# A mixture-of-experts layer on one core: expert rows through tables in DRAM instead of one-hot matmuls

## The reference

```
logits = xf @ w_router
vals, idx = lax.top_k(logits, 2)
gates = sum(one_hot(idx, 8) * softmax(vals))
for e in range(8):
    out += gates[:, e:e+1] * ((silu(xf @ wg[e]) * (xf @ wu[e])) @ wd[e])      # inner width 3584
```

## Time and profile before

| | |
|---|---|
| median of 3 runs | 1660.03 us (1659.11 to 1660.29) |
| profiled execution, first to last instruction (span) | 1658.4 us |
| PE busy | 95% of the span |
| DVE, ACT, POOL busy | 72%, 58%, 3% |
| mean granted clock of PE | 0.974 |
| moved by DMA | 431.69 MB, mean 260 GB/s |

### The profile page before, as it was taken

The page is one execution under the profiler, slowest core; times in us unless marked ns, Lnnn a source line. Parts: engine busy times, 40 slices in busy tenths (PEclk is TensorE's granted clock), DMA queues, the critical chain, the costliest instruction groups (busy, mean ns, idle before and its releaser), DMA issues.

```text
span 1658.4 us, 22346 instructions
## 1 busy us (share of the span) xinstructions
PE 1580.2 (95%) x8017; PEld 1306.1 (79%) x8017; DVE 1192.4 (72%) x1088; ACT 961.0 (58%) x932; POOL 56.3 (3%) x90
## 2 busy tenths in 40 slices
PE   4899899999799699999999999999999999999996
PEld 3687699999687478878888888887887887887885
DVE  3635455544545468879879879879878887987886
ACT  4534444334335357757766766766766775776674
POOL 2010000000210100000000000000000000000001
PEclk9999899999799779999999999999999999999999
DMA  8433254440524059979979978979997997997992
GB/s 326 148 127 118 86 183 172 159 172 29 229 105 165 0 218 367 370 274 351 370 280 346 364 298 334 365 292 339 365 356 273 365 366 280 349 365 283 349 365 107
DMA packets 60618, 431.69 MB, mean 260 GB/s; under 512 B 6913, under 2 KB 7327, under 8 KB 8975
## 3 DMA queue, kind: packets, MB, share of 16 engines
q1 hardware_dynamic: 59966, 429.53, 68.6%
q0 software_dynamic: 608, 1.56, 0.3%
HBM read 428.60 MB, written 2.74 MB: 260 GB/s over the span
## 4 chain that ended last, share of the span: by engine, by line
PE 92%; DVE 4%; ACT 2%; issue 1%; POOL 1%; DMA 0%; POOLq 0%; DVEq 0%; SPq 0%; ACTq 0%
PE bank L265 28%; PE bank L267 27%; PE bank L266 27%; PE bank L1437 4%; PE bank L1461 1%; PE bank L1111 1%; DVE wlo L253 1%; ACT whi L249 1%; PE bank L1481 1%; ACT junk L438 1%; PE bank L1483 1%; DVE hT_lo L700 0%; ACT hT_hi L447 0%; DVE xn L693 0%; PE bank L1238 0%
## 5 line engine op out<-in xcount | busy, mean ns | idle before, releaser
L253 DVE TENSOR_TENSOR wlo<-raw,whi 128x2048 fp32r<-128x2048 f32 x402 | 920.5, 2291 | 209.2 <-ACT whi L249 208.9
L249 ACT ACTIVATE whi<-raw 128x2048 fp32r<-128x2048 f32 x402 | 769.0, 1915 | 189.7 <-PE bank L267 189.3
L265 PE MATMUL bank<-whi,gT_hi 128*128 128x512 f32 x896 | 365.1, 408 | 0.0
L267 PE MATMUL bank<-whi,gT_lo 128*128 128x512 f32 x896 | 355.4, 397 | 0.0
L266 PE MATMUL bank<-wlo,gT_hi 128*128 128x512 f32 x896 | 354.1, 395 | 0.0
L267 PEld LDWEIGHTS bank<-whi,gT_lo 128*128 128x128 f32 x896 | 169.2, 189 | 39.3
L265 PEld LDWEIGHTS bank<-whi,gT_hi 128*128 128x128 f32 x896 | 169.9, 190 | 36.0
L266 PEld LDWEIGHTS bank<-wlo,gT_hi 128*128 128x128 f32 x896 | 169.9, 190 | 34.8
L265 PE MATMUL bank<-whi,eT_hi 128*128 128x512 f32 x448 | 177.4, 396 | 1.0 <-DVE eT_lo L991 1.0
L266 PE MATMUL bank<-wlo,eT_hi 128*128 128x512 f32 x448 | 177.2, 396 | 0.0
L267 PE MATMUL bank<-whi,eT_lo 128*128 128x512 f32 x448 | 176.3, 393 | 0.0
(11 more groups left out here) (187 smaller groups left out, 1632.6 us busy)
## 6 DMA issues: line engine op xcount, KB each, us to landing
raw<-in_stream SPq DMA_DIRECT2D x402, 1024.0 KB, 4.8
table<-in_table SPq DMA_DIRECT2D x2, 896.0 KB, 14.4
const<-in_const SPq DMA_DIRECT2D x1, 1192.0 KB, 21.8
stage<-in_mem SPq DMA_DIRECT2D x2, 512.0 KB, 5.1
x<-in_x_prompt SPq DMA_DIRECT2D x1, 1024.0 KB, 11.2
out_y_prompt<-xm SPq DMA_DIRECT2D x2, 512.0 KB, 2.6
out_mem_k<-kv POOLq DMA_DIRECT2D x2, 256.0 KB, 4.3
out_mem_v<-kv POOLq DMA_DIRECT2D x2, 256.0 KB, 4.3
```

The source lines that it names most:

```text
L249: nc.scalar.activation(whi[:, slot % SPL, :], raw[:, slot, :], ACT.Copy).then_inc(hi_ready, 1)
L253: nc.vector.tensor_tensor(wlo[:, slot % SPL, :], raw[:, slot, :], whi[:, slot % SPL, :].bitcast(F), ALU.subtract).then_inc(lo_ready, 1)
L265: nc.tensor.matmul(out, a_hi, b_hi, start=start, stop=False, **kw)
L267: return nc.tensor.matmul(out, a_lo, b_hi, start=False, stop=stop, **kw)
```

## The change

Two tables in DRAM are added: `x_slots` (8 experts x 384 slots, rows of 1024 floats, 12.58 MB) and `y_slots` (7 x 128 + 128 rows, 4.19 MB).

- At the start of the dense up stage ACT issues two transfers that write zeros over both tables.
- Before the experts DVE computes for each token its two rows (`key`, `best`, `to_row`), and POOL writes the normed token rows to them by six indirect transfers (`x_spread`).
- At the start of an expert ACT loads the next expert's 128 rows (`rows_e`). The gather for experts 1 to 7 becomes eight transposes of `rows_e` (`turn_rows`); the first expert's stays one with matmuls.
- The output of experts 0 to 6 is copied from PSUM to `y_rows` (ACT the left half, DVE the right half) and stored by ACT (`save_y`). The scatter and its adds stay for expert 7 alone.
- During expert 7 POOL fetches each token's two rows back by indirect transfers (`got`), and DVE adds them, weighted, after steps 4, 5, 6 and 9, 10, 11 (`add_got`). The small computations for this (`choices`, `rows_of_choices`) stand on DVE in expert 6.

The diff, cut to its core:

```diff
@@ build
+        x_slots = nc.dram_tensor("x_slots", [NE * SLOTS, D], F, kind="Internal").ap()
+        y_slots = nc.dram_tensor("y_slots", [Y_ROWS + P, D], F, kind="Internal").ap()
...
@@ gpsimd
+            pool.wait_ge(zero_filled, 32)
+            pool.wait_ge(S["xm_out"], 2)
+            pool.wait_ge(S["xm_tile1_out"], 1)
+            pool.wait_ge(S["to_row_out"], 1)
+            for j in range(2):
+                for t in range(3):
+                    r = ROWS[t]
+                    nc.gpsimd.indirect_dma_start(
+                        out=x_slots, out_offset=bass.IndirectOffsetOnAxis(ap=to_row[0:r, j, t:t + 1], axis=0),
+                        in_=xm[0:r, t, :], in_offset=None).then_inc(x_spread, 16)
...
+                    if j == 0:
+                        pool.wait_ge(S["from_row_out"], r + 1)
+                        pool.wait_ge(y_saved, r * (16 * (NE - 1)) + 16 * NE)
+                    else:
+                        pool.wait_ge(S["got_added"], r * 6 + 3)
...
+                        nc.gpsimd.indirect_dma_start(
+                            out=got[0:rr, t, :], out_offset=None, in_=y_slots,
+                            in_offset=bass.IndirectOffsetOnAxis(ap=from_row[0:rr, j, t:t + 1], axis=0))\
+                            .then_inc(got_in, 16)
@@ scalar
                 if l == 0:
+                    act.wait_ge(S["zero_set"], 1)
+                    blank = zero.rearrange("p (a d) -> p a d", a=1)
+                    nc.scalar.dma_start(x_slots.rearrange("(p a) (b d) -> p (a b) d", p=P, b=4),
+                                        blank.to_broadcast([P, NE * SLOTS // P * 4, D // 4])).then_inc(zero_filled, 16)
+                    nc.scalar.dma_start(y_slots.rearrange("(p a) (b d) -> p (a b) d", p=P, b=4),
+                                        blank.to_broadcast([P, 4 * NE, D // 4])).then_inc(zero_filled, 16)
...
+                def y_left_of(w, cb):
+                    act.wait_ge(chunk_used, cb + EXP_CH)
+                    act.wait_ge(y_saved, w * 16 + 16)
+                    nc.scalar.activation(y_rows[:, 0:512], bank[6][:, :], ACT.Copy).then_inc(S["y_out"], 1)
+
+                def save_y(e, w):
+                    act.wait_ge(S["y_out"], w * 2 + 2)
+                    nc.scalar.dma_start(y_slots[y_slot_rows(e), :], y_rows[:, :]).then_inc(y_saved, 16)
...
+                    if not last:
+
+                        act.wait_ge(x_spread, 16 * 6)
+                        nc.scalar.dma_start(rows_e[:, :], x_slots[slot_rows(e + 1), :]).then_inc(rows_in, 16)
...
-                    act.wait_ge(chunk_used, cb + EXP_CH)
-                    y_hi_of()
+                    y_left_of(w, cb)
                     hi(cb, lap, 3 * s + 2)
+                    save_y(e, w)
@@ vector
+            V.memset(xm[:, 2, :], 0.0)
...
+            for t in range(3):
+                last = V.tensor_tensor(key[:, t, :], posm[:, t, :], base[:, :], ALU.add)
+            link(last)
+            link(V.tensor_tensor(key[:, :, :], key[:, :, :], mask[:, :, :], ALU.mult))
+            for t in range(3):
+                last = V.max(best[:, t, :], key[:, t, :])
+            link(last)
+            for j in range(2):
+                last = V.tensor_scalar(to_row[:, j, :], best[:, :, j], -1.0, None, ALU.add)
+            last.then_inc(S["to_row_out"], 1)
...
+                def add_got(j, t):
+
+                    rr = ROWS[t]
+                    if t == 0:
+                        dve.wait_ge(got_in, r * 96 + 48 * (j + 1))
+                    V.scalar_tensor_tensor(out=x[0:rr, t, :], in0=got[0:rr, t, :], scalar=at_gate[0:rr, j, t:t + 1],
+                                           in1=x[0:rr, t, :], op0=ALU.mult, op1=ALU.add).then_inc(S["got_added"], 1)
...
+                def y_right_of(w, cb):
+                    dve.wait_ge(chunk_used, cb + EXP_CH)
+                    dve.wait_ge(y_saved, w * 16 + 16)
+                    V.tensor_copy(y_rows[:, 512:D], bank[7][:, :]).then_inc(S["y_out"], 1)
...
-                    y_lo_of(q)
+                    y_right_of(w, cb)
                     lo(cb, 3 * s + 2)
                     turned_of(g0, s)
                     lo(cb, 3 * s + 3)
-                    add(q, e, 0, 1)
...
-                    add(q, e, 2, 3)
...
-                    add(q, e, 4, 5)
@@ tensor
+                def turn_rows(b):
+
+                    for k in range(4 * b, 4 * b + 4):
+                        last = T.transpose(bank[b][:, (k % 4) * P:(k % 4 + 1) * P], rows_e[:, k * P:(k + 1) * P], ident)
+                    last.then_inc(S["gat_done"], 1)
...
-                    pe.wait_ge(S["sel_out"], q + 2)
-                    pe.wait_ge(S["selT_out"], q + 1)
-                    pe.wait_ge(S["x_added"], 6 * q + 2)
-                    gather(0)
+                    pe.wait_ge(rows_in, w * 16 + 16)
+                    turn_rows(0)
                     gate_up(cb, 3 * s, s + 1, 0, j)
                     turn_hidden(g0, s)
-                    gather(1)
+                    turn_rows(1)
...
-                    turn_sel(q + 1)
+                    if isinstance(e, int):
+                        pe.wait_ge(S["sel_out"], r * 2 + 2)
+                        turn_sel()
...
-                    scatter(q, j, 0, 1)
+                    pe.wait_ge(S["y_out"], w * 2 + 2)
                     down(cb, g0, 3 * s + 2, s)
                     s = STEPS + 1
                     gate_up(cb, 3 * s, s + 1, 0, 1 - j)
-                    scatter(q, j, 2, 3)
...
-                    scatter(q, j, 4, 5)
```

More of the change, by code:

```diff
@@ L61 @@
 FAR = 8192.0
+SLOTS = MAX_ROUNDS * P
+Y_ROWS = (NE - 1) * P
+SETTLES = 7
 NEVER = -3.0e38
@@ L230, in build @@
             "selT_done", "selT_out", "gat_done", "gat_hi", "gat_lo", "esilu", "eh_out", "eT_done", "eT_hi_out", "eT_out",
-            "y_hi_out", "y_out", "scat_done", "x_added", "fin_out")}
+            "y_hi_out", "y_out", "y_last_out", "scat_done", "x_added", "fin_out",
+            "to_row_out", "from_row_out", "got_added", "zero_set", "ticked", "settled")}
+        zero_filled, x_spread, rows_in, y_saved, got_in = (
+            sem(n) for n in ("zero_filled", "x_spread", "rows_in", "y_saved", "got_in"))
         stored, final_stored = sem("stored"), sem("final_stored")
@@ L886, in _ @@
             V.memset(mask[:, :, :], 0.0)
+            V.memset(gate[:, :, :], 0.0)
+            V.tensor_scalar(base[:, :], slots[:, 0:NE], float(SLOTS), 1.0, ALU.mult, ALU.add)
+            V.tensor_scalar(shelf[:, :], slots[:, 0:NE], float(P), None, ALU.mult)
             V.memset(posm[:, :, :], -FAR)
@@ new lines, in rows_of_choices @@
+                def rows_of_choices():
+                    V.tensor_scalar(in_round[:, :, :], at_pos[:, :, :], 0.0, None, ALU.is_ge)
+                    for j in range(2):
+                        last = V.tensor_scalar(kept[:, j, :], best[:, :, j], float((NE - 1) * SLOTS), None, ALU.is_le)
+                    settle(last)
+                    settle(V.scalar_tensor_tensor(out=kept[:, :, :], in0=at_pos[:, :, :], scalar=float(P), in1=kept[:, :, :],
+                                                op0=ALU.is_lt, op1=ALU.mult))
+                    settle(V.tensor_tensor(kept[:, :, :], kept[:, :, :], in_round[:, :, :], ALU.mult))
+                    settle(V.scalar_tensor_tensor(out=at_row[:, :, :], in0=at_spot[:, :, :], scalar=-float(Y_ROWS),
+                                                in1=kept[:, :, :], op0=ALU.add, op1=ALU.mult))
+                    V.tensor_scalar(from_row[:, :, :], at_row[:, :, :], float(Y_ROWS), None, ALU.add)\
+                        .then_inc(S["from_row_out"], 1)
@@ L1019, in expert @@
                 def expert(e, j, last):
-                    q, cb, g0 = regs(e)
-                    if not last:
-                        select(e + 1)
-                    with V.Fori(0, STEPS // 2 - 2) as p:
-                        step(cb, g0, 2, p)
-                        step(cb, g0, 3, p)
+                    q, w, cb, g0 = regs(e)
+                    if last:
+                        for s in range(2, STEPS - 2):
+                            step(cb, g0, s)
+                            if s in (4, 5, 6):
+                                add_got(0, s - 4)
+                            if s in (9, 10, 11):
+                                add_got(1, s - 9)
+                    else:
+                        if isinstance(e, int):
+                            choices()
+                            select(e + 1)
+                        with V.Fori(0, STEPS // 2 - 2) as p:
+                            step(cb, g0, 2, p)
+                            step(cb, g0, 3, p)
                     s = STEPS - 2
```

153 lines of the change are left out of this document (108 added, 45 removed).

## The result

The changed kernel takes **1604.46 us** (median of 4 runs, 1603.04 to 1607.63), the kernel before 1659.57 beside it: ratio 0.9675, 95% interval 0.966 to 0.9691. The forecast was 1651, a gain of 9; the gain is 55. All sums here go by these spans.

A forecast was written before the change was run, and what follows sets the result against it. PE, busy 95% of the span, was taken to bound the kernel. Seams and the other terms except the zeros gave -67.8 us (1592 us); the zeros added 59, making 1651 us; 8-in-10 range 1586 to 1672.

The forecast's parts named there:

- Step 6: Zero fills in the dense up stage: 61 us long, ACT held 58, PE idle 56, 3 of clock; together +59 us.
- The rival "hidden": Both zero fills issue in half a microsecond each and ACT goes on; 1592 us (1586 to 1600), chance 0.24.
- the forecast's own case: ACT held by the zeros at 0.042 to 0.070 us per run; 1633 to 1662 us, forecast 1651, chance 0.48.
- The 1630: Sum with the zeros at line rate: fill 40 us at 419 GB/s, hold 37; said to lie within the forecast's case.
- Step 1: Seams of experts 0 to 5: 11.89 us goes, transposes 1.04 and waits 0.5 come; -10.35 each, -62.1 us.
- Steps 2 and 4: Expert 6's seam, with small DVE operations half covered: -8.5 us; expert 7's six `add_got`, 0.4 over each: +2 us.
- Step 3: Ahead of expert 0: `turn_sel` off the chain -0.93, small operations +1.2, memset 0.5; together +0.8 us.
- Step 5: `rows_e` loads and `y_rows` stores on ACT, and POOL's twelve indirect transfers: no cost.

The follow-up runs named there:

- e2: The changed kernel with both tables in one tensor, so that one transfer of 16384 runs writes all zeros; 1576.79 us.
- e3: The changed kernel with the two fills in the other order, `y_slots` (4 MB) first and `x_slots` (12 MB) second; 1582.76 us in a single run.
- e1: The changed kernel with the `y_slots` fill issued some 115 us later, after 18 of the 22 up chunks; 1575.94 us.
- e12: The kernel before with unused buffers added and `selT` moved behind `eT`, so the experts' matmul buffers lie at the changed kernel's addresses; 1653.15 us.
- e11: The kernel before, without tables, with the third tile of every matmul gather padded with zeros and contracted over 128 rows instead of 32; 1631.52 us.
- e7: e1 with expert 6's choices, selection and row numbers on DVE spread a few at a time behind its steps; 1575.73 us.
- e10: e7 with the memset of `xm`'s third tile moved ahead of the wait for the router's matmuls; 1574.92 us.
- e5: The changed kernel with the first gather's third tile contracted over its 32 real rows again instead of all 128; 1610.69 us.

## Why the prediction was wrong

**Step 6, the zeros, is the step that failed**: +59 forecast, +31 measured. It has two terms, and both were too long. *How long*: I took 0.060 us per 1 KB run; it is 0.042, the lower end of the bounds and what the earlier trace rows had said. That moves the fill from 61 to 43 us, and the hold by the forecast's rule from 58 to about 40: 18 of the 28 us by which the step was too long. The upper end had been worked out from packets mixed with other loads, where I put a whole difference on the short ones. *How ACT is held*: "held until nearly all runs are taken" is wrong for any one transfer (e2: 1.17 us for all of it) and right only for what is issued behind it. With two fills it is the first fill's 12 MB that count, not the 16: 28.5 us, which with the clock is the other 10. The order of the two issues alone is worth 22 us (e3, one run), and the place of the second 29 (e1). The chain behind it came as foretold: ACT, DVE's `wlo`, PE 27.9 us idle after 2 us in hand, 1.4 us of clock where I had 3.

**The rival "hidden"** had given as its reason that the number of commands counts. It was nearer on the mechanism for the first issue (0.68 us) and wrong for the second. Its price, 1592, is what a kernel without the hold would have had by my other steps; with the hold gone e1 had 1576. It was this rival that took the range down to 1586, so that the range holds the result by luck, over a path that did not happen; the forecast's own case ended at 1633. (The 1630 that I called within that case lay 3 us below it.)

**Step 1, seams of experts 0 to 5**: -10.35 each, measured -11.82 (-70.9 for six, against -62.1). The interval from expert 0's first silu to expert 1's shrank by 8.88 only, as a scatter falls behind the next expert's first silu; the scatter of expert 5 is thus in the interval of expert 6. The seam itself went from 11.89 to 0.9, -10.99; of the charged 0.5 for new waits nothing came, and the transposes took 0.88 rather than 1.04. The other 0.8 us per expert lie in no part of the change as I read it: they are the place of `eT` and its neighbours (e12). The total of the earlier trace rows was right, yet 3.06 of it were the price of mixed tile heights (e11), which a cheaper edit removes too.

**Steps 2 and 4, the seam of expert 6 and expert 7**: -8.5 and +2 forecast. By first silus, expert 6's interval shrank by 132.03 - 124.64 = 7.39, less than the 11.82 of its neighbours. I let half of 3 us be covered, but the block stood in one piece ahead of `eh`, so nearly all was paid, 4.4 us with the row numbers and `turn_sel`; in pieces most is covered (e7: 1.6). For step 4 I had 0.4 over for each of six `add_got`, which is 2.5 and not the +2 that I wrote. All six show: between silus the steps take 9.06 to 9.10 us, and the last, shorter interval 7.24 where e12, with the same steady step and no `add_got`, has 6.69. That is 0.57 over each, +3.4. The scatter of expert 6 (-2.82) and 14 shorter steps (-1) pay it back, as the -0.17 of the last stretch says.

**Step 3, ahead of expert 0**: +0.8 forecast, +1.87 measured to the gather. Some 0.8 of it is the memset's, where I took 0.5: e11 has it without `key` and `to_row`, and from the last `hT_lo` to the gather takes 12.25 us instead of 11.44. Its way is not the one I had: it puts `nfirst` behind the start of POOL's product, which then holds it (e10), so that all that follows `nfirst` comes after the product. The other 1.06 are the operations from `key` to `to_row` (1.2 forecast). And then came -9.78 that I had not seen, since I read the padding as a cost on DVE and never asked what full tiles do on PE. The gather makes 7.14 of it and `turn_sel` 0.93; the rest is the matmuls behind, which before still ran at the low clock (0.43 us each until 599 us).

**Step 5** held: `rows_e` loads were issued in 0.36 us and landed in 7.9, and nothing waited for them. POOL issued the six scatters between 609.62 and 620.43 us, 0.85 to 2.44 each, 20 us before the first load of `rows_e` at 640.9.

So the kernel was faster for the reason given, the seams, and its cost was where I put it. By the spans the forecast was -67.8 + 59 = -8.8 and the result -52.5. Of the 43.7 between them, 28 are the zeros (59 against 30.95), 8.7 the stretch ahead of expert 0's first silu (+0.8 against 1.87 - 9.78), and 6.9 the eight experts (-68.6 against -75.5), where the places of the buffers alone give 112 steps x 0.066 = 7.4 (12 matmuls, 0.0055 each).

## What to carry to other kernels

A large fill costs its issuer almost nothing when the queue is empty; the next transfer on the same queue pays, until the former is almost done. So never issue two large ones back to back from an engine that also computes: put them in one transfer, or the small one first, or the second much later. And before pricing matmuls from a trace, see which tile heights they mix: the same gather cost half as much again only because every third one had 32 rows. When a stretch of unedited instructions changes its pace, look at the addresses before looking for a cause in the program.

## What the runs showed of the hardware that I had not expected

- One transfer of 16384 runs was issued in 1.17 us, of 12288 in 0.68; the next on that queue was held 28.5 us, until by estimate 100 to 130 runs an engine were left. SP's issues were not held (0.33 us each in e1 and e2).
- The granted clock at the first gather depends on the tile heights. With 48 full tiles it was 0.52 from 610 to 615 us and 1.00 from 615; with every third of 32 rows it stayed at 0.50 (the lower level, 1.2 GHz) from 605 to 625 us in e5, though PE was busy nearly all of it. In windows of e5 (busy PE, PEclk, DMA share, GB/s):

```profile
605.00:610.00 5.00, 5.00 (x18) 0.50 0.63 228
...
615.00:620.00 5.00, 4.40 (x14) 0.50 1.01 423
```

- Each excursion from 128 to 32 rows and back cost 0.385 us at full clock, the matmul behind it included.
- A matmul's pace moved by 2% with the addresses of buffers alone, 7.0 us over the kernel (e12).
- A DVE operation on 128 x 2 took 0.17 us ahead of a POOL product on 128 x 1024 and 1.39 to 2.17 us where it began while that ran; in all ten such traces it ended 0.02 or 0.03 us after the product.
- The fill and the weights' loads slowed each other without PE feeling it: in e1 the loads issued from 205 to 255 us landed after 7.6 us (median) instead of 4.8 and the fill took 59 us instead of 35, and PE was busy without a gap.
